# A decoder step on one core: every cached row and page gets its own slot in memory that dies tile by tile, and two rounds and two folds move behind other products

## The reference, cut to what matters

```python
h = h + 0.5 * rms(swiglu_1(rms(h)))
qa, ka, va, qb, kb, vb, ga, gb = split(rms(h) @ w_in)     # 13 + 8 column blocks
oa = dilated windows over k/v, three groups, 4 heads      # prompt: own k/v; sample: cache rows
ob = stick breaking, 8 heads                              # sample: 2 pages of 128 cached rows each
h = h + rms((sigmoid(ga) * (oa @ p_a) + sigmoid(gb) * (ob @ p_b)) @ w_o)
h = h + 0.5 * rms(swiglu_2(rms(h)))
```

## Time and profile before

| | |
|---|---|
| median of 3 runs | 1338.21 us (1337.44 to 1342.02) |
| the profiled execution | 1344.6 us |
| its span, first to last instruction | 1342.8 us |
| TensorE busy | 1292.7 us, 96% |
| VectorE, ScalarE, GpSimd busy | 45%, 30%, 0% |
| mean granted TensorE clock | 0.983 of full speed |

### The profile page before, as it was taken

How to read it: one execution, slowest core, us unless ns; L and a number is a source line. 1 busy time by engine, 2 the same in 40 slices (tenths; PEclk the granted TensorE clock), 3 DMA queues, 4 the chain that set the end, 5 groups by cost and what they waited for, 6 DMA issues and landing times.

```text
span 1342.8 us, 24585 instructions
## 1 busy us (share of the span) xinstructions
PE 1292.7 (96%) x10532; PEld 1246.3 (93%) x10532; DVE 598.1 (45%) x934; ACT 401.9 (30%) x660; POOL 4.9 (0%) x31
## 2 busy tenths in 40 slices
PE   7999999999998999999999978999899999999996
PEld 6999999999997999888888877999899999999996
DVE  6343434332348322454467722576644343342335
ACT  6222221212215332333345532244522222222221
POOL 0000000000000000000000000000000000000000
PEclk9999999999999999899999988999999999999998
DMA  5222222222222232111121256421132222222211
GB/s 192 67 91 94 94 94 94 94 87 87 87 87 77 95 125 79 58 36 75 48 95 39 89 167 192 160 95 63 42 117 94 94 94 89 81 78 107 92 56 64
DMA packets 30217, 123.13 MB, mean 92 GB/s; under 512 B 4442, under 2 KB 12658, under 8 KB 18418
## 3 DMA queue, kind: packets, MB, share of 16 engines
q1 hardware_dynamic: 30146, 122.09, 26.6%
HBM read 115.39 MB, written 6.67 MB: 91 GB/s over the span
## 4 chain that ended last, share of the span: by engine, by line
PE 90%; DVE 5%; ACT 2%; DMA 1%; issue 1%; DVEq 1%; SPq 0%; POOL 0%; POOLq 0%; ACTq 0%
PE bank L1186 27%; PE bank L1187 26%; PE bank L1188 26%; PE bank L1211 2%; PE bank L1372 2%; PE bank L1334 1%; DVE w_lo L854 1%; PE bank L1413 1%; PE bank L1360 1%; PE bank L1420 1%; PE bank L1430 1%; DVEq L848 1%; DVE f L895 1%; ACT w_hi L517 1%; DVE rinv L891 1%
## 5 line engine op out<-in xcount | busy, mean ns | idle before, releaser
L1186 PE MATMUL bank<-u_hi,w_hi 128*128 128x260 f32 x2144 | 619.9, 289 | 14.4 <-DVE u_lo L883 11.1
L1188 PE MATMUL bank<-u_hi,w_lo 128*128 128x260 f32 x2144 | 609.5, 284 | 0.0
L1187 PE MATMUL bank<-u_lo,w_hi 128*128 128x260 f32 x2144 | 609.4, 284 | 0.0
L1186 PEld LDWEIGHTS bank<-u_hi,w_hi 128*128 128x128 f32 x2144 | 407.9, 190 | 31.3 <-issue 25.2
L1187 PEld LDWEIGHTS bank<-u_lo,w_hi 128*128 128x128 f32 x2144 | 408.0, 190 | 0.1
L1188 PEld LDWEIGHTS bank<-u_hi,w_lo 128*128 128x128 f32 x2144 | 408.1, 190 | 0.0
L517 ACT ACTIVATE w_hi<-raw 128x2048 fp32r<-128x2048 f32 x87 | 166.4, 1913 | 324.7 <-PE bank L1188 324.7
L854 DVE TENSOR_TENSOR w_lo<-raw,w_hi 128x2048 fp32r<-128x2048 f32 x51 | 116.8, 2290 | 229.0 <-ACT w_hi L517 212.4
L1186 PE MATMUL bank<-hid_hi,w_hi 128*128 128x260 f32 x704 | 199.4, 283 | 0.0
L1187 PE MATMUL bank<-hid_lo,w_hi 128*128 128x260 f32 x704 | 199.0, 283 | 0.0
L1188 PE MATMUL bank<-hid_hi,w_lo 128*128 128x260 f32 x704 | 198.8, 282 | 0.0
(11 more groups left out here) (174 smaller groups left out, 1127.1 us busy)
## 6 DMA issues: line engine op xcount, KB each, us to landing
raw<-w_stream SPq DMA_DIRECT2D x90, 1024.0 KB, 4.9
raw<-w_stream SPq DMA_DIRECT2D x8, 768.0 KB, 4.3
h<-x_t SPq DMA_DIRECT2D x8, 260.0 KB, 6.3
y_t<-h SPq DMA_DIRECT2D x8, 260.0 KB, 2.5
block<-kb_pool SPq DMA_DIRECT2D x8, 256.0 KB, 3.6
ring<-kb_pool SPq DMA_DIRECT2D x8, 256.0 KB, 3.2
ring<-vb_pool SPq DMA_DIRECT2D x8, 256.0 KB, 4.1
block<-vb_pool SPq DMA_DIRECT2D x8, 256.0 KB, 3.0
```

What stands on the lines that cost most here:

```text
L1186: pe.matmul(out_of(b), w, hi_x, start=first, stop=False)
L1187: pe.matmul(out_of(b), w, lo_x, start=False, stop=False)
L1188: return pe.matmul(out_of(b), v, hi_x, start=False, stop=last)
```

## The change

It does six things.

1. Slots. Row tiles 4 to 7 get `slot_a[0:4]`, the 16 key pages 16 slots (`slot_a[4:8]`, `slot_b`, `slot_c`, `ring`), the value pages 16 slots. `slot_a` and `slot_b` lie over `q_b`, `k_b` and others, cut so that a slot lies inside tiles that the prompt's work has done with after 4, 8, 12 or 16 steps of scores.
2. SP's order. Cached rows 0 to 3 and key pages 0 to 5 are issued between the weight loads while the prompt's stick breaking still runs, on waits for `b_scored`. After `b_out` 16 come row tiles 4 to 7, then key pages 6 to 11, chunk GB+3, pages 12 to 15, and values in pieces as their slots come free. Each round has one semaphore step (`keys_used`, `page_used`) for all its tiles.
3. TensorE's order. Item 18 runs before the wait for `s_zero`. The second rows' round moves from behind item 19 to behind item 20; of the four rounds of key pages the first moves from behind item 20 to 19, the third from 22 to 23, the fourth from 23 to 24. `sample_turn_a` moves from behind item 22 to 24, the values of A each one item later, the first fold from 28 to 29, `sample_values_b(0)` from 28 to 31.
4. The second round of `sample_values_b` leaves item 31 and goes between PA's products 11 and 12; the fold of round 0 goes behind PA's product 1, that of round 1 between PA and PB.
5. VectorE clears `s1` and `s2` at the start of step 15, ahead of the low part of step 14 and of `lo` of chunk 54, and makes `lo` of chunk 55 ahead of the softmax.
6. ScalarE's pieces for the samples move with these, by one to three items.

```diff
+    slot_a = [Placed(nc, work + 2048 * i)(f"slot_a{i}", [P, 512]) for i in range(8)]
+    slot_b = [Placed(nc, work + at)(f"slot_b{i}", [P, 512]) for i, at in enumerate((20640, 22688, 24800, 26848))]
+    slot_c = [Placed(nc, work + at)(f"slot_c{i}", [P, 512]) for i, at in enumerate((28960, 31040, 33120, 35168))]
+    slot_d = [Placed(nc, R + at)(f"slot_d{i}", [P, 512]) for i, at in enumerate((54784, 52736))]
+    key_rows = ring + slot_a[0:4]
+    key_page = [slot_a[6], slot_b[0], slot_a[7], slot_b[1], slot_b[2], slot_b[3], slot_a[4], slot_a[5]] + slot_c + ring
+    value_page = slot_c[2:4] + ring + slot_d + slot_a
...
             load_next(GB)
-            load_next(GB + 1)
             sp.wait_ge(v_turned, 13)
...
-            for x in range(4):
-                load_keys_a(x)
+            load_keys_a(0, 4)
+            sp.wait_ge(kb_out, 32)
+            sp.wait_ge(b_scored, 8)
+            load_key_pages(0, 2)
+            load_next(GB + 1)
+            sp.wait_ge(b_scored, 16)
+            load_key_pages(2, 4)
             load_next(GB + 2)
+            sp.wait_ge(b_scored, 24)
+            load_key_pages(4, 5)
+            sp.wait_ge(b_scored, 32)
+            load_key_pages(5, 6)
+            sp.wait_ge(vb_out, 32)
             sp.wait_ge(b_out, 16)
-            load_key_pages(0, 2)
-            for x in range(4, 8):
-                load_keys_a(x)
-            load_key_pages(2, 12)
+            load_keys_a(4, 8)
+            load_key_pages(6, 12)
             load_next(GB + 3)
-
-            sp.wait_ge(page_used, 8)
+            sp.wait_ge(keys_used, 1)
+            load_key_pages(12, 16)
+            sp.wait_ge(page_used, 2)
             sp.dma_start(va_1[:], va_cache1).then_inc(va_in, 16)
-            load_key_pages(12, 16)
+            sp.wait_ge(keys_used, 2)
...
+            sp.wait_ge(page_used, 3)
+            load_value_pages(0, 2)
             load_next(GB + 4)
-            load_value_pages(0, 12)
+            sp.wait_ge(page_used, 4)
+            load_value_pages(2, 6)
+            sp.wait_ge(s_turned, 1)
+            load_value_pages(6, 7)
+            sp.wait_ge(va_in, 96)
+            load_value_pages(7, 8)
+            sp.wait_ge(va_used, 1)
+            load_value_pages(8, 12)
             load_next(GB + 5)
             load_value_pages(12, 16)
...
-            pe.wait_ge(s_zero, 2)
-            pe.wait_ge(qz_made, 20)
             for j in range(2, 16):
                 gate_item(16 + j)
-                if j < 4:
-                    sample_keys_a(j - 2)
-                elif j < 8:
-                    sample_keys_b(j - 4)
-                if j == 6:
+                if j == 2:
+                    pe.wait_ge(s_zero, 2)
+                    pe.wait_ge(qz_made, 20)
+                    sample_keys_a(0)
+                if j == 3:
+                    sample_keys_b(0)
+                if j == 4:
+                    sample_keys_a(1)
+                if j == 5:
+                    sample_keys_b(1)
+                if j == 7:
+                    sample_keys_b(2)
+                if j == 8:
+                    sample_keys_b(3)
                     sample_turn_a()
...
-                if j in (12, 15):
-                    sample_values_b((j - 12) // 3)
-            fold_turn(1, s1)
+                if j == 15:
+                    sample_values_b(0)
...
                 if x == 2:
-                    fold_turn(2, s2)
+                    fold_turn(1, s1)
+                if x == 12:
+                    sample_values_b(1)
...
+            fold_turn(2, s2)
             for x in range(16):
...
-                if x == 0:
+                if x == 2:
                     pe.wait_ge(s_lo, 6)
```

More of the change, by code:

```diff
@@ L142, in step_program @@
     m_at = late.at
-    ring = [late(f"ring{i}", [P, 512]) for i in range(3)] + [Placed(nc, spare)("ring3", [P, 512])]
+    ring = [late(f"ring{i}", [P, 512]) for i in range(3)] + [Placed(nc, spare + 96)("ring3", [P, 512])]
     late = Placed(nc, work)
@@ L148, in step_program @@
     suffix = Placed(nc, sqa_at)("suffix", [P, 2, 520])
[L149 to L152, removed]
+    slot_a = [Placed(nc, work + 2048 * i)(f"slot_a{i}", [P, 512]) for i in range(8)]
+    slot_b = [Placed(nc, work + at)(f"slot_b{i}", [P, 512]) for i, at in enumerate((20640, 22688, 24800, 26848))]
+    slot_c = [Placed(nc, work + at)(f"slot_c{i}", [P, 512]) for i, at in enumerate((28960, 31040, 33120, 35168))]
+    slot_d = [Placed(nc, R + at)(f"slot_d{i}", [P, 512]) for i, at in enumerate((54784, 52736))]
+    va_23 = Placed(nc, work)("va_23", [83, DEC, 256])
+    va_1 = Placed(nc, work + 8192)("va_1", [P, DEC, 256])
+    key_rows = ring + slot_a[0:4]
+    key_page = [slot_a[6], slot_b[0], slot_a[7], slot_b[1], slot_b[2], slot_b[3], slot_a[4], slot_a[5]] + slot_c + ring
+    value_page = slot_c[2:4] + ring + slot_d + slot_a
     s_a = Placed(nc, R + 54784)("s_a", [P, 2, 211])
@@ L230, in step_program @@
         b_lo = sem("b_lo")
-        ring_in = [sem(f"ring_in{i}") for i in range(4)]
-        page_in = [sem(f"page_in{i}") for i in range(8)]
+        key_in = [sem(f"key_in{i}") for i in range(8)]
+        page_in = [sem(f"page_in{i}") for i in range(16)]
+        keys_used = sem("keys_used")
         page_used = sem("page_used")
-        ring_used = sem("ring_used")
         va_in = sem("va_in")
@@ L425, in page, with load_keys_a @@
                 sp.dma_start(slot[:], pool_t[bass.ds(r, 1)].rearrange("a p c -> (a p) c")).then_inc(sem_in, 16)
[L427 to L431, removed]
+            def load_keys_a(x0, x1):
+                for x in range(x0, x1):
+                    sp.dma_start(key_rows[x][:, 0:422], ka_cache[x]).then_inc(key_in[x], 16)
             def load_key_pages(y0, y1):
                 for y in range(y0, y1):
[L436 to L440, removed]
+                    page(kb_pool, y, key_page[y], page_in[y])
             def load_value_pages(y0, y1):
                 for y in range(y0, y1):
[L445 to L451, removed]
+                    page(vb_pool, y, value_page[y], page_in[y])
             load_next(GB)
-            load_next(GB + 1)
             sp.wait_ge(v_turned, 13)
@@ L1094, in _ @@
                     b_chain(p + 1)
+                else:
+                    for score in (s1, s2):
+                        dve.memset(score[:], 0.0).then_inc(s_zero, 1)
                 if p:
@@ L1139, in _ @@
             lo(GB + 5)
-            for r in range(2):
-                fold_low(2 + 2 * r, (s1, s2)[r], ob_hi, ob_lo, 4, r)
+            fold_low(2, s1, ob_hi, ob_lo, 4, 0)
             for x in range(16):
@@ L1461, in sample_keys_a @@
                                            qz_a[:, 2 * g + t, 4 * rnd + j, :],
-                                           ring[j][:, t * 211 + k0:t * 211 + k1], start=t == 0, stop=t == 1)
-                            if g == 2 and t == 1:
-                                mm.then_inc(ring_used, 1)
+                                           key_rows[4 * rnd + j][:, t * 211 + k0:t * 211 + k1], start=t == 0,
+                                           stop=t == 1)
+                mm.then_inc(keys_used, 1)
             def sample_keys_b(z):
@@ L1474, in sample_keys_b @@
                     for j in range(4):
-                        y = 4 * z + j
-                        slot = ring[j] if y >= 8 else blocks[4 + y]
                         mm = pe.matmul(s2[32 * j:32 * j + BH, col:col + P], qz_b[:, t, 4 * rnd + j, :],
-                                       slot[:, t * P:(t + 1) * P], start=t == 0, stop=t == 3)
-                        if t == 3:
-                            mm.then_inc(ring_used if y >= 8 else page_used, 1)
+                                       key_page[4 * z + j][:, t * P:(t + 1) * P], start=t == 0, stop=t == 3)
+                mm.then_inc(page_used, 1)
             def sample_turn_a():
```

60 lines of the change are left out of this document (24 added, 36 removed).

## The result

The changed kernel takes 1321.22 us (median of 4 runs, 1319.56 to 1325.08) against 1339.08 for the kernel before on the same chip (4 runs, 1337.44 to 1342.02): ratio 0.9868, 95% interval 0.984 to 0.9897. The forecast was 1321.3.

A forecast was written before the change was run, and what follows sets the result against it. TensorE, busy 96%, bounds the kernel by its work plus standstills and slow clock. Idle 11.41 plus slow clock 5.72 is 17.13 us, less 0.2 wait is 16.9, off median 1338.21 gives 1321.3 us; range 1318 to 1328.

The forecast's parts named there:

- Idle pieces, 11.41 us: Four TensorE idle pieces between 776 and 836 us would go: 3.31, 3.18, 4.40 and 0.52 us.
- Slow clock, 5.72 us: Half-speed TensorE pieces during or behind the three large idle pieces would go with them, saving 5.72 us.
- The larger clock term by the rule, 8.5 us: Rival: penalty is half of all low clock time, about 17 us; gain 20.1 us, 1318.1 us; chance 0.05.
- The laid out order: TensorE's same work in new order from 776.34 us, checked against each supplier; no slack came out negative.
- Item 31: On TensorE, items, rounds and transposes laid out from 776.34 us would bring its end to about 827.7 us.
- The memsets: On VectorE, done near 772.2 us and wanted at 779.3, cover 7 us; moving them costs nothing.
- Rows 4 to 7: Loads issued from 776.4 us, ready at 782.5, wanted at 787.3; slack 4.8 us.
- chunk 58: Weight load with thinnest slack: issued near 819.2 us, landed 824.2 to 826.7, wanted 828.0; slack 1.3 to 3.8 us.
- PA's fifth product: TensorE would wait there 0 to 0.6 us for the first bank to be free; 0.2 us taken.
- the rival of returning waits: Rival: dense DMA and full SP queue use up slacks, or unprofiled losses are smaller; 1323 to 1330 us; chance 0.24.
- The third stall: TensorE idle 4.40 us at 810.10 to 814.50 for key pages 12 to 15, waiting for pages 8 to 11's use.
- Profile and median: The profiled run's 6.4 us over the median was placed outside these stalls, so all 16.9 us came off the median.

The follow-up runs named there:

- e1: Kernel before, with matmuls that nobody reads put where TensorE stood idle at three places, waits kept; median 1336.62 us, ratio to before 0.9986.
- e4: Changed kernel with rows 4 to 7 issued behind key pages 6 to 11 instead of ahead; median 1328.45 us, ratio to the kernel before 0.9913.
- e6: Changed kernel with weight chunk 58 issued behind value pages 12 to 15 instead of ahead; median 1324.33 us, ratio to the kernel before 0.9892.
- e10: Changed kernel with item 18 back behind the wait and the memsets behind the low part of chunk 54; median 1327.72 us, ratio to before 0.99.
- e5: Changed kernel with only the two memsets put back behind the low part of chunk 54; median 1320.92 us, ratio to the kernel before 0.9867.
- e3: Changed kernel with no key page issued before the prompt's last step ends, pages 0 to 11 following rows 4 to 7; median 1325.37 us, ratio 0.99.
- e7 to e9: Changed kernel with TensorE order put back: second values' round; second rows' round; both plus third and fourth rounds of pages; medians 1320.63, 1323.12, 1321.26 us.
- e2: Kernel before with only the two memsets moved ahead on VectorE and item 18 ahead of their wait; median 1334.68 us, ratio to before 0.997.
- e11: Kernel before run once more, nothing edited, for a second trace; 1338.89 us, one run.

## Why the prediction was right, step by step

**Idle pieces, 11.41 us.** Right, and steady: 11.4 and 11.8 us in two traces, 0.1 after. This is the larger and the sure part.

**Slow clock, 5.72 us.** Right for the trace it was read from: TensorE's busy time fell by 5.95 us at the same work. In the second trace of the kernel before it is 4.0. The mechanism is shown by e1, where filling the idle alone kept the clock at 1.00. What the prediction did not say is that this term belongs to an execution and not to the kernel; a sum of 15.7 to 17.4 would have been the honest form. The median difference, 17.9 us, has an interval of 13.8 to 21.4 by the ratio and holds both ends. That the forecast of 1321.3 lies 0.1 us from the median of 1321.22 is therefore luck: the forecast gain was 16.9 us from a median of 1338.21, the measured one 17.9 from 1339.08.

**The larger clock term by the rule, 8.5 us.** Wrong here, as forecast. The Trainium skill, "TensorE: Matmul & The Clock Gate", section Terms, takes half of all throttled time; the trace does not agree: between the first trace and the changed kernel, which has no low piece left, TensorE's busy time fell by 5.95 us, and with every low piece removed at once and the time of the stalls still there, e1's stage fell by 4.6 us. By these numbers the low clock cost nothing while TensorE had nothing to do. The sum of this rival was also 0.4 us too high: 11.41 + 8.5 - 0.2 is 19.7, not 20.1.

**The laid out order.** Item 31 was put 51.4 us behind the end of the prompt's last step and ended 50.95 behind it. The memsets ended 4.1 us before that step (4.1 predicted). Rows 4 to 7 had 5.2 us of slack (4.8 predicted), chunk 58 had 1.7 (1.3 to 3.8), PA's fifth product a wait of 0.08 us (0.2). No supplier was late, so the rival of returning waits did not come true. How near it lies e4 and e6 show: two groups of loads exchanged on SP cost 6.2 or 2.1 us.

**Which part earned it.** The prediction did not rank the parts. The runs do in part, each by one trace: item 18 and the memsets ahead together 4.8 us (e10), of which either alone seems to bring nearly all (e5 and the memsets' row); the early pages 4.0 us (e3); the rows first behind the last step 6.2 us against the other order (e4); the later places of the second rows' round, of two rounds of pages and of the second values' round nothing (e7 to e9). These do not sum to 17.4, since each was taken out with the rest in place. The third stall, 4.4 us for key pages 12 to 15, was never put back by itself, and no run takes the slots away and keeps SP's order: that both of these are gone in the changed kernel is shown, what each is worth is not. Value pages were the next thing late: e1, e2 and the second trace of the kernel before have a wait of 1.1 to 1.5 us for them, which the changed kernel has not.

**Profile and median.** The prediction placed the 6.4 us between the profiled execution and the median elsewhere than in the stalls. Mostly right: the slow clock at 546 to 557 us is in that trace and not in the second, whose stretch begins 6.2 us earlier with stalls of the same size. About 1.7 us of it was in the stage: 2.0 more of slow clock and 0.3 less of idle.

## What to carry to other kernels

Where one queue issues all loads and slots take turns, write down for each load when it is issued, when it is wanted and what the difference is. A slot of its own lets a load be issued earlier; see that the queue then gives it that place, and ahead of which others. Price a stall as its idle time, and add the slow clock behind it as a range from zero up. Before moving compute around to hide transfers, move the transfers, then try the old order again: here the new order of the rounds that were put back was not needed.

## What the runs showed of the hardware that I had not expected

- The length of an idle piece did not decide by itself whether the clock fell. Behind 3.18 us idle it was 0.50 in one trace, behind 3.0 us of the same wait it stayed 1.00 in another (e11), behind 2.8 us of it (e2) and behind 2.4 us of a different one (e3) it fell to 0.50. The price of the same 3.3 us stall was 2.4 us of clock once and 1.5 us another time (e10).
- Behind six pages, four row tiles took 7.7 us from first issue to last copy against 5.8 with none ahead (e4, one trace of each); the pages' own issue time comes on top. A 1 MB chunk took 6.7 us to land in the changed kernel and 5.3 in e6, issued 5.2 us later.
